# One level of Strassen's scheme for both projections of a hybrid attention and convolution layer

## The reference

```python
def reference(x, norm_w, w_in, sinks, conv_w, conv_b, w_out, rel_bias, final_norm_w):
    for l in range(DEPTH):
        hn = rmsnorm(x, norm_w[l])
        proj = jnp.einsum('bsd,de->bse', hn, w_in[l])
        q, k, v, g_attn, h, c_gate, b_gate, g_conv = jnp.split(proj, SPLIT_POINTS, axis=-1)
        attn = swa_sink_attention(q, k, v, sinks[l], rel_bias)
        conv = short_gated_conv(h, c_gate, b_gate, conv_w[l], conv_b[l])
        mixed = jnp.concatenate([attn * jax.nn.silu(g_attn),
                                 conv * jax.nn.silu(g_conv)], axis=-1)
        x = x + jnp.einsum('bse,ed->bsd', mixed, w_out[l])
    return rmsnorm(x, final_norm_w)
```

## Time and profile before

| | before |
|---|---|
| median of three runs | 1544.08 us (1544.03 to 1544.28) |
| span of the profiled execution | 1542.4 us |
| PE busy | 1511.6 us (98%) |
| DVE busy | 738.0 us (48%) |
| ACT busy | 372.5 us (24%) |
| POOL busy | 113.3 us (7%) |
| DMA | 165.53 MB, mean 107 GB/s |

### The profile page before, as it was taken

The page is one execution under the profiler, slowest core; times in us unless marked ns, Lnnn a source line. Parts: engine busy times, 40 slices in busy tenths (PEclk is TensorE's granted clock), DMA queues, the critical chain, the costliest instruction groups (busy, mean ns, idle before and its releaser), DMA issues.

```text
span 1542.4 us, 19005 instructions
## 1 busy us (share of the span) xinstructions
PE 1511.6 (98%) x6979; PEld 1260.6 (82%) x6979; DVE 738.0 (48%) x930; ACT 372.5 (24%) x687; POOL 113.3 (7%) x128
## 2 busy tenths in 40 slices
PE   4999999999999999999999999999999999999997
PEld 4888888888888888888888888888888888888886
DVE  7621111355455637547464465646557444454431
ACT  6321111111111212212122221222123333323321
POOL 4300000000000000000000000000000011121110
PEclk9999999999999999999999999999999999999999
DMA  7343332221233222323223232233223645346433
GB/s 275 56 145 102 102 102 88 75 75 59 91 92 86 72 85 79 87 80 92 68 80 90 74 89 81 68 92 82 83 77 113 213 159 173 131 169 210 160 118 121
DMA packets 209105, 165.53 MB, mean 107 GB/s; under 512 B 60032, under 2 KB 175808, under 8 KB 207280
## 3 DMA queue, kind: packets, MB, share of 16 engines
q1 hardware_dynamic: 184560, 132.73, 28.8%
q0 software_dynamic: 7616, 28.19, 4.9%
q10 hardware_dynamic: 16896, 4.20, 1.2%
HBM read 132.70 MB, written 32.37 MB: 107 GB/s over the span
## 4 chain that ended last, share of the span: by engine, by line
PE 94%; DVE 2%; DMA 1%; issue 1%; ACT 0%; SPq 0%; POOL 0%; POOLq 0%; ACTq 0%; DVEq 0%
PE banks L1104 70%; PE banks L1209 18%; PE banks L1228 2%; PE banks L1164 1%; PE banks L1188 1%; PE banks L1178 1%; DVE arena L784 1%; DMA resid<-in_x_dram 1%; PE banks L1090 1%; DVE act_lo L790 0%; DMA stage<-in_norm_w_dram 0%; DVE w_lo L769 0%; DVE arena L780 0%; PE banks L1173 0%; DVE arena L1032 0%
## 5 line engine op out<-in xcount | busy, mean ns | idle before, releaser
L1104 PE MATMUL banks<-act_hi,w_hi 128*128 128x512 f32 (+1 forms) x1632 | 507.7, 389 | 4.1 <-DVE w_lo L769 4.1
L1104 PE MATMUL banks<-act_lo,w_hi 128*128 128x512 f32 (+1 forms) x1632 | 502.9, 386 | 0.0
L1104 PE MATMUL banks<-act_hi,w_lo 128*128 128x512 f32 (+1 forms) x1632 | 502.2, 386 | 0.0
L769 DVE TENSOR_TENSOR w_lo<-w_raw,w_hi 128x512 fp32r<-128x512 f32 x312 | 231.3, 746 | 485.8 <-ACT w_hi L594 485.8
L1104 PEld LDWEIGHTS banks<-act_hi,w_lo 128*128 128x128 f32 x1632 | 307.7, 189 | 62.1
L1104 PEld LDWEIGHTS banks<-act_lo,w_hi 128*128 128x128 f32 x1632 | 307.8, 189 | 62.0
L1104 PEld LDWEIGHTS banks<-act_hi,w_hi 128*128 128x128 f32 x1632 | 302.1, 189 | 60.1 <-issue 3.6
L594 ACT ACTIVATE w_hi<-w_raw 128x512 fp32r<-128x512 f32 x312 | 195.0, 629 | 616.1 <-PE banks L1104 471.6
L1209 PE MATMUL banks<-w_hi,act_hi 128*128 128x512 f32 x448 | 174.5, 390 | 0.4 <-DVE arena L923 0.2
L1209 PE MATMUL banks<-w_hi,act_lo 128*128 128x512 f32 x448 | 174.3, 389 | 0.0
L1209 PE MATMUL banks<-w_lo,act_hi 128*128 128x512 f32 x448 | 174.3, 389 | 0.0
(11 more groups left out here) (91 smaller groups left out, 853.2 us busy)
## 6 DMA issues: line engine op xcount, KB each, us to landing
w_raw<-in_w_in_dram SPq DMA_DIRECT2D x200, 256.0 KB, 2.9
w_raw<-in_w_out_dram SPq DMA_DIRECT2D x112, 256.0 KB, 3.5
qkv_park<-stage POOLq DMA_DIRECT2D x20, 512.0 KB, 3.7
arena<-in_x_dram SPq DMA_DIRECT2D x8, 1024.0 KB, 6.3
q_cur<-qkv_park SPq DMA_DIRECT2D x64, 128.0 KB, 2.8
resid<-in_x_dram SPq DMA_DIRECT2D x32, 256.0 KB, 4.0
arena<-mix_park SPq DMA_DIRECT2D x20, 256.0 KB, 3.9
gate_park<-arena POOLq DMA_DIRECT2D x8, 512.0 KB, 4.1
```

The lines of the kernel that those rows point to most:

```text
L769: dve.tensor_tensor(w_lo[:, slot, :], w_raw[:, slot, :], w_hi[:, slot, :], ALU.subtract).then_inc(w_lo_ready, 1)
L1104: op = pe.matmul(proj[par][:, lo // N, lo % N:lo % N + hi - lo], w, a[:, k, lo:hi], start=(k == 0 and w is wh and a is act_hi), stop=(k == ...
```

## The change

It is a rewrite. **The products.** Each projection is cut into blocks of 1024 output columns by all 1024 tokens by all 2048 of the contraction: block 0 the attention's gate, block 1 queries, keys and values (1280 columns, five tiles wide per product), blocks 2 to 5 the convolution (256 columns of each of the four kinds), blocks 6 and 7 the two halves of the output projection. A block is computed as seven half-size products instead of eight, in the order 1, 2, 3, 6, 7, 5, 4 (the Winograd form), each over half of the contraction: 8 steps, a step being one slice of the contraction for all 4 (or 5) tiles, 12 (or 15) matmuls at L1517. That makes 8 blocks of 56 steps, 448 steps. **The sums of operands.** The four sums of weights of a block (`s1` to `s4`) are formed in place in `raw` by POOL. The four sums of x (`t1` to `t4`) are formed in place in `z`, by DVE for block 0 and by POOL for blocks 6 and 7. Split sums go into a ring of weights (`w_ring`, 5 slots) and one of x (`x_ring`, 6 or 5). The 56 slots of x of block 0 are stored to `x_park` (512 KB each) and loaded again for each of blocks 1 to 5. **The sums of products.** ACT copies product 1 out of PSUM (`base`), DVE adds the others into four fp32 tiles `e` (`sums`, eight additions per output tile). **The rest.** Silu is `g * (1 + tanh(g/2)) / 2`, so the reciprocals over 1024 columns are gone. A unit of attention now lies in six steps: queries by keys at phase 0, transposes ahead of phase 3, probabilities by values ahead of phase 5. The residual is added by POOL through the same two buffers, the first half of y is parked in DRAM, and the last norm's rows are finished behind the last products.

```diff
-            def quarter(q, count, par, spans=((0, N), (N, S))):
-                pe.wait_ge(w_lo_ready, count + 1)
+            def wait_operands(n):
+                b, p, kt = place(n)
+                pe.wait_ge(w_lo_ready, n + 1)
+                if b in ON_CHIP:
+                    pe.wait_ge(x_lo_ready, x_index(n) + 1)
+                else:
+                    pe.wait_ge(x_loaded[X_SLOT[n]], 16 * X_TURN[n])
...
+            def turn_probs(u):
+                pe.wait_ge(shifted, u + 1)
...
+                pe.wait_ge(probs_ready, u + 1)
...
+                u, ph = unit_at(s)
+                if 0 <= u < UNITS:
+                    if ph == 0:
+                        queries_by_keys(u)
+                    elif ph == 3:
+                        turn_probs(u)
+                    elif ph == 5:
+                        probs_by_values(u)
+                step(s)
...
+            def s1(b, kt):
+                wait_raw(b, 1, kt)
+                wait_raw(b, 1, HK + kt)
+                pool.tensor_tensor(raw[:, 1, kt, :], raw[:, 1, kt, :], raw[:, 1, HK + kt, :], ALU.add).then_inc(s1_ready, 1)
+
+            def s2(b, kt):
+                pool.wait_ge(w_lo_ready, at(b, 1, kt) + 1)
+                pool.wait_ge(s1_ready, 8 * b + kt + 1)
+                pool.tensor_tensor(raw[:, 0, kt, :], raw[:, 1, kt, :], raw[:, 0, kt, :], ALU.subtract).then_inc(s2_ready, 1)
...
+            def w_hi(n):
...
+                if n >= NW:
+                    act.wait_ge(step_done, n - NW + 1)
+                act.activation(w_ring[:, n % NW, 0, :], raw[:, c, h * HK + kt, :], ACT.Copy).then_inc(w_hi_ready, 1)
...
+            def w_lo(n):
...
+                dve.tensor_tensor(w_ring[:, n % NW, 1, :], raw[:, c, h * HK + kt, :], w_ring[:, n % NW, 0, :],
+                                  ALU.subtract).then_inc(w_lo_ready, 1)
...
+                elif p == 6:
+                    dve.tensor_tensor(e3, e1, ps, ALU.add)
+                    dve.wait_ge(sum_ready, sum_count(b, 3, t))
+                    dve.tensor_tensor(e2, e2, ps, ALU.add).then_inc(sum_ready, 1)
...
+            def load_resid(r):
...
+                if r >= 2:
+                    sp.wait_ge(resid_added, r - 1)
...
+                n = s + LW
+                if n < STEPS:
+                    w_lo(n)
...
+                if kt == HK - 1 and p != 1 and not (b == OUT1 and p == 4):
+                    for t in range(WIDE[b]):
+                        sums(b, p, t)
+                u, ph = unit_at(s)
+                if ph == 1 and 0 < u <= UNITS:
+                    gate_output(u - 1)
+                elif 0 <= u < UNITS:
+                    if ph == 0:
+                        shift_logits(u)
+                    elif ph == 2:
+                        normalise(u)
+                    elif ph == 4:
+                        turn_p_lo(u)
...
+            for i in range(4):
+                y_variance(i)
+            for t in range(4):
+                finish_1(t)
+            for t in range(4):
+                sums(OUT1, 4, t)
+                y_variance(4 + t)
+                finish_0(t)
```

2067 lines of the change are left out of this document (1214 added, 853 removed).

## The result

The changed kernel takes **1595.38 us** (1593.48 to 1596.52, four runs) beside 1544.05 us for the kernel before: 1.0336 times as long, 95% interval 1.0321 to 1.035. It is 3.4% slower. The forecast was 1521.6 us, faster by 1.5%, and the range ended at 1590. Rival B, "the port decides", had 1602 us, which is near for reasons given at the end.

A forecast was written before the change was run, and what follows sets the result against it. It took the number of matmuls on PE alone as the bound. Its terms, 44 + 3 + 1262.4 + 47.5 + 12 + (14 + 20 + 12 + 16) + 25 + 10 + 54, gave a 1519.9 us span, forecast 1521.6 us, range 1445 to 1590.

The forecast's parts named there:

- Rival B: DVE and POOL alternate on the port, 1.15 us per DVE instruction, 76 us in output blocks; 1602 us, chance 0.25.
- PE's part: PE throughout: 5544 matmuls at the old rate take 1262.4 us, 180.3 us less; the 32 units take 47.5 us.
- start and block 0: Up to block 0's end, 200.0 us: start unchanged at 44 us, 3 us showing from DVE's added subtractions.
- waits in blocks 2 to 5: Attention stage, 74 us: late normalisations 14, sums 20, convolution pieces 12, port 16, first unit 12.
- waits in the output blocks: Blocks 6 and 7: DVE's splits and POOL's sums share the port, and POOL enters the last block late; 25 us.
- clock in these stages: Whole kernel: some five waits longer than 3 us lower PE's clock, costing 10 us.
- behind the last product: Tail after the last matmul: late residual, DVE and POOL in turns, last norm's rounds, final store; 54 us.
- the first unit: After block 1: keys and values pass through one staging buffer while PE reaches unit 0; 12 us with block 1's boundaries.
- The port's share: Attention stage: POOL's reads delay six two-input DVE instructions per unit by 0.5 or 0.25 us each; 16 us.
- Rival A: Whole kernel: DVE keeps its lead and POOL's instructions fall into gaps; 81 us less, 1441 us, chance 0.20.
- Rival C: Stream of x: loads and stores at only 230 GB/s are not hidden, 56 us more, 1578 us; chance 0.05.
- the three signs named for being wrong: Attention waits under 30 or over 110 us, a split not lengthened by POOL, or a tail under 40 us.

The follow-up runs named there:

- e1: Changed kernel with all of POOL's sums of weights and of x cut to one column, so left out: 1521.04 us.
- e6: Changed kernel with attention lists reordered: normalisation earlier, transposes of probabilities in phase 4, products with values at phase 0 of the next unit: 1528.9 us.
- e4: Changed kernel with two calls swapped in DVE's list: a unit's normalisation in phase 1, the previous unit's gated output in phase 2: 1556.29 us.
- the filler: Changed kernel with 8 unused matmuls on PE ahead of each of the 32 waits for the probabilities: 1604.43 us.
- e5: Changed kernel with the 64 sums of x of the two output blocks moved from POOL to DVE: 1576.9 us.
- e12: Kernel with reordered start loads and POOL's powers put ahead, block 0's 32 weight sums then cut to one column: 1578.96 us.

## Why the prediction was wrong, point by point

**PE's part was right.** 5544 matmuls, 0.2277 us each where nothing waits (24 in 5.49 us), the 32 units, and block 1 within 0.8 us.

The rest of the sum, term by term (us; "waits" here is what a stage is longer than its products, units and loss at 1.2 GHz):

| term | forecast | measured | difference |
|---|---|---|---|
| start and block 0 | 200.0 | 220.3 | +20.3 |
| block 1 | 191.3 | 192.1 | +0.8 |
| waits in blocks 2 to 5 | 74 | 87.2 | +13.2 |
| waits in the output blocks | 25 | 52.7 | +27.7 |
| clock in these stages | 10 | 33.7 | +23.7 |
| behind the last product | 54 | 40.1 | -13.9 |

**The output blocks are the step that failed most.** The sum had 25 us: it added DVE's and POOL's time on the port over a whole block, 165 us for a stretch of 153, and let the lead of four steps take up to 8. Measured: 52.7 us, 62.5 with the clock, and e1 shows POOL's sums to be the cause of 40.5 of these 62.5. Of the 42 waits 11 lie between 1262 and 1299 us and 29 between 1373 and 1490. There a step takes 3.40 us for 2.73, and where POOL rests PE cannot make up for it, since 2.73 is its own time. A mean over the block hides that. The forecast also gave each split a quarter or half microsecond, since "POOL can give way"; the two alternate, and DVE pays 1.1 us each time. I took the traces' two overlaps for single pairs when both were already of full length (and only the second is of an instruction that reads two tensors).

**The clock is the second.** It stood at 10 us for the whole kernel, "some five waits longer than 3 us" at 2 us each. The price was right, 33.7 us for 17 stretches, 2.0 each; the count was not. It came from one example of 2.9 us; the wait of 2.30 us above already cost 1.6, and of the 29 waits for the probabilities alone ten last 2.3 us or more. Three runs bear it out in blocks 2 to 5: the loss fell with the waits by 15 us in e6, 11 in e4 and 14 with the filler.

**The attention's waits were close, in part by luck.** The sum had 62 us for late normalisations, sums, convolution pieces and port, and 12 for the first unit. By the profile's count it is 63.6 and 12.7. But the count leaves 0.25 us out of each wait, and the forecast's prices were spacings: a plain unit costs 0.42 + 0.25 us for 0.44, and all of them 87.2 for 74. The port's share there was 16; without POOL's sums the wait for the probabilities falls by 15.8 and the stage by 27.1, 9 of it clock. The single parts of the 62 were not measured.

**Rival B** had the mechanism, 1.15 us per instruction, and the sign. Its sizes were too large as the forecast's were too small: 76 us for the output blocks where 52.7 came, and 45 for the port in the attention, where e1 has 27 with the clock in it. That its 1602 us lie so near to 1595 is luck: it has the forecast's terms for the start and the clock, which were 20 and 24 us too small and made up for it.

The rule of the Trainium skill ("Perfetto Trace Analysis", section "Optimizing Scalar/DVE Operations") that moving work between POOL and DVE may not help, as they share a read port, was borne out in its reason: POOL's sums cost 74 us (e1). In the one direction that was tried, 64 of them from POOL to DVE, the move did help, by 18.5 us (e5). The other rule of the Trainium skill, "SBUF — State Buffer", section "Who interferes with whom", is now borne out in its second half as well: sums with one operand in PSUM take 678 ns with POOL at work and without.

**The start.** "The start stays at 44 us", and 3 for block 0; measured 20.3 us more, 7.3 us of block 0 lost at 1.2 GHz among them. The forecast costed 32 subtractions on DVE, but not the store of x behind the loads, for which PE waits 14.3 us, nor that POOL's eight pairs of sums begin only when some 16 MB have landed and product 3 stands behind them. e12 shows the second chain behind the first; two orders of loads only exchanged them.

**The tail** was 14 us shorter than the 54. Its last residual came before the last product's end instead of 7 us behind it, in part because the product was late itself, by the 5.25 us that PE waited for DVE's last splits. The turns were there as forecast: 1024 columns in 3.36 us beside POOL, 1.28 alone.

**Rival A** (DVE keeps its lead, 1441 us) did not come about; the fastest version is at 1482.8. **Rival C** did not happen: PE never waits for the stream of x in the changed kernel.

Of the three signs named for being wrong, none fired: the attention's waits lay between 30 and 110 us, the splits were lengthened, the tail was 40.1 us (one of under 40 would have counted). They watched the mechanisms, which were right; the sizes of port, clock and start were off, and the chance of "slower", 0.31, was too small for a sum that left 22 us of margin over so many terms.

## What to carry to other kernels

Where matmuls are traded for work on DVE and POOL, add up the two engines' time on instructions that read two operands from SBUF as if they were one engine, and compare it with PE's time product by product, not over a block: here 165 us in 153 looked like 12 too many and cost 26. For the waits that PE has, add what the clock takes behind the long ones: here 24 us behind 76, about a third as much again. Read a wait from the starts of the matmuls, since the count was 0.25 us short each time. And before moving work, look at the order of the lists: here two calls that changed places were worth 39 us, as much as half of the port.

## What the runs showed of the hardware

- With both at it, DVE and POOL alternate one for one: 1.70 us for each pair of a DVE instruction (0.60 alone) and a POOL instruction (1.27 alone). POOL loses 0.43 us by it, DVE 1.1.
- POOL's writes alone do not take part: a memset of 512 columns runs beside a split of 0.69 us.
- Shorter waits than the one in the trace of before (2.9 us) cost clock: behind 2.30 us, 24 matmuls took 7.34 us instead of 5.72, at a granted clock of 0.57 over the first 4 us. In blocks 2 to 7 of the changed kernel, 17 of 18 waits of 2.30 us or more have a stretch at 1.2 GHz beside them, 2.0 us lost for each, and no wait of up to 1.83 us has.
- The profile's count of PE's waits is 0.25 us short for each: two steps of 2.73 us started 3.39 us apart with 0.41 us counted between them.
